# 32 of 512 latent tokens moved from the dense expert products to gathered rows, routing cut into steps, and some VectorE operands read from PSUM

## The reference, cut to what matters

```python
q = (xb @ w_pq).reshape(TOK_BLOCK, 8, 2, 128)
s = einsum('thcd,hcnd->thcn', q, sub_keys)              # 2 x 128 scores for each head
s1, i1 = top_k(s[:, :, 0], 16); s2, i2 = top_k(s[:, :, 1], 16)
top_s, pos = top_k(all 256 sums s1 + s2, 16)            # an expert is i1 * 128 + i2
g = softmax(top_s)
a = gelu(einsum('thk,td->thk', u_exp[eidx], xb))
y = einsum('thk,thkd->td', g * a, v_exp[eidx])
```

## Time and profile before

| what | before |
|---|---|
| median of three runs | 4217.21 us |
| the profiled execution | 4209.3 us |
| its span in the profile | 4207.5 us |
| TensorE busy | 4015.6 us |
| VectorE busy | 2789.8 us |
| GpSimd busy | 2321.4 us |
| ScalarE busy | 1751.2 us |
| moved by DMA | 921.99 MB |

### The profile page before, as it was taken

How to read it: one execution, slowest core, us unless ns; L and a number is a source line. 1 busy time by engine, 2 the same in 40 slices (tenths; PEclk the granted TensorE clock), 3 DMA queues, 4 the chain that set the end, 5 groups by cost and what they waited for, 6 DMA issues and landing times.

```text
span 4207.5 us, 57280 instructions
## 1 busy us (share of the span) xinstructions
PE 4015.6 (95%) x21230; PEld 3364.7 (80%) x21230; DVE 2789.8 (66%) x4311; ACT 1751.2 (42%) x3014; POOL 2321.4 (55%) x1112
## 2 busy tenths in 40 slices
PE   7978999999999899999989999999999989999997
PEld 5757898888888788877769989888888878887875
DVE  3773239889898566566643322989989867676665
ACT  3264324756657322322231132374655732222223
POOL 1101225676767666666643322576676767666664
PEclk9999999999999999999999999999999999999999
DMA  5303235867768988888844312486776898888884
GB/s 207 113 1 126 86 101 165 280 224 244 261 222 284 315 280 288 277 282 286 297 145 180 102 59 88 146 294 216 256 251 226 277 321 275 284 286 276 289 295 157
DMA packets 385364, 921.99 MB, mean 219 GB/s; under 512 B 29296, under 2 KB 161136, under 8 KB 370800
## 3 DMA queue, kind: packets, MB, share of 16 engines
q1 hardware_dynamic: 310432, 647.48, 46.0%
q0 software_dynamic: 73728, 268.47, 18.8%
q10 hardware_dynamic: 976, 3.15, 0.2%
HBM read 776.64 MB, written 142.34 MB: 218 GB/s over the span
## 4 chain that ended last, share of the span: by engine, by line
PE 32%; issue 30%; POOL 29%; DVE 4%; DMA 3%; ACT 1%; DVEq 0%; POOLq 0%; ACTq 0%
PE PS L736 21%; POOL SL L427 17%; POOL ROWS L434 9%; PE PS L544 5%; PE PS L728 4%; POOL SL L418 3%; DMA ROWS<-u_exp,EI 2%; PE PS L748 2%; DMA ROWS<-v_exp,EI 1%; PE PS L695 1%; DVE OH L1196 1%; DVE ROWS L1205 1%; DVE EQ L1177 0%; DVE EQ L1173 0%; ACT SH L963 0%
## 5 line engine op out<-in xcount | busy, mean ns | idle before, releaser
L427 POOL TENSOR_TENSOR SL<-RW,SH 128x1024 fp32r<-128x1024 f32 x512 | 1409.3, 2753 | 922.7 <-ACT SH L963 901.1
L963 ACT CAST SH<-RW 128x1024 fp32r<-128x1024 f32 x512 | 537.4, 1050 | 1063.8 <-PE PS L736 537.7
L736 PE MATMUL PS<-HH,SH 128*128 128x512 f32 x2048 | 815.9, 398 | 28.3 <-POOL SL L427 28.2
L748 PE MATMUL PS<-WH,SH 128*128 128x512 f32 x2048 | 811.2, 396 | 11.0 <-DVE WL L1255 5.6
L748 PE MATMUL PS<-WL,SH 128*128 128x512 f32 x2048 | 809.4, 395 | 0.0
L748 PE MATMUL PS<-WH,SL 128*128 128x512 f32 x2048 | 809.4, 395 | 0.0
L736 PE MATMUL PS<-HL,SH 128*128 128x512 f32 x2048 | 801.5, 391 | 0.0
L736 PE MATMUL PS<-HH,SL 128*128 128x512 f32 x2048 | 801.4, 391 | 0.0
L1211 DVE SCALAR_TENSOR_TENSOR ACC<-ROWS,AA,ACC 128x1024 f32<-128x1024 f32 x256 | 369.7, 1444 | 528.8 <-DMA ROWS<-v_exp,EI 522.3
L418 POOL TENSOR_TENSOR SL<-RW,SH 128x1024 fp32r<-128x1024 f32 x84 | 202.6, 2416 | 816.5 <-ACT SH L788 816.5
L1196 DVE TENSOR_TENSOR OH<-CO,PK 128x1024 f32<-128x1024 f32 x256 | 575.7, 2290 | 96.1 <-PE PS L728 88.0
(11 more groups left out here) (161 smaller groups left out, 5203.4 us busy)
## 6 DMA issues: line engine op xcount, KB each, us to landing
RW<-u_blk SPq DMA_DIRECT2D x256, 512.0 KB
RW<-v_blk SPq DMA_DIRECT2D x256, 512.0 KB
gate_acts<-GE SPq DMA_DIRECT2D x256, 256.0 KB
router_weights<-GT SPq DMA_DIRECT2D x64, 1024.0 KB, 5.2
GB<-router_weights SPq DMA_DIRECT2D x32, 2048.0 KB, 12.3
GL<-gate_acts SPq DMA_DIRECT2D x256, 256.0 KB
RW<-wstream SPq DMA_DIRECT2D x100, 512.0 KB
AW<-wpairs SPq DMA_DIRECT2D x40, 1024.0 KB, 5.1
```

Source lines behind the costliest of these rows:

```text
L427: nc.gpsimd.tensor_tensor(SL[:, r % 2], RW[:, r % RAW], SH[:, r % 2].bitcast(F32), ALU.subtract).then_inc(raw_used, 1)
L736: last = mm(PS[:, n % 2], w[:, n % 2, j], a[:, j, 0:NS], start=(j == 0 and q == 0), stop=(j == DJ - 1 and q == 2))
L748: last = mm(PS[:, dj], w[:, k % 2, dj], a[:, k], start=start, stop=stop)
L963: nc.scalar.copy(SH[:, r % 2], RW[:, r % RAW]).then_inc(hi_done, 1)
```

## The change

- The first 32 latent tokens leave the dense path: `u_product`, `v_products`, gelu, weights and their transfers work on columns 32 to 511, and there are 120 quads instead of 128.
- These tokens are gathered. They are laid out four times over the 128 partitions (32 tokens x 4 groups), so that 32 gathers (`PG`) of 128 rows fetch their 128 picks; a layer now has 160 gathers in each stage (`NPICK`) instead of 128, the new ones first. ScalarE's queue issues eight small DMAs (`few_tokens`) that spread their indices and gates. The v rows add up in `HTOK`; after the last v product TensorE folds the four groups into columns 0 to 31 (`FOLD`), and VectorE waits for that (`folded`).
- Routing becomes a generator of 26 steps that VectorE runs between one-hots and picks, over the blocks of `ROUTE_SPAN`. Quads and gathers are spread evenly (`QUAD_BLOCK`, `PICK_AT`, `VPICK_AT`).
- The numbers 0 to 127 (`IOTA_PS`), the prompt tokens (`HTOK_PS`) and the slot's indices (`IF`) now lie in PSUM, where VectorE reads them. ScalarE's copy of the prompt tokens ahead of the first block goes away; a copy of the 32 tokens comes after `high(0)`.

The core of the diff:

```diff
+NG = 32
+ND = NS - NG
+GQ = P // NG
+PG = PICKS // GQ
+NPICK = PICKS + PG
+NQ = ND // 4
+NTG = ND // TG
...
-OH_BLOCKS = 16
-LEAD, BETWEEN = (20, 20), 12
-SEG = [[LEAD[l] + t * (OH_BLOCKS + BETWEEN) for t in range(TT - 1)] for l in range(DEPTH)]
-OH_AT = [{SEG[l][t] + j: t * OH_BLOCKS + j for t in range(TT - 1) for j in range(OH_BLOCKS)} for l in range(DEPTH)]
-PICKS_AT = [{11: 0, **{SEG[l][t]: t for t in range(1, TT - 1)}} for l in range(DEPTH)]
-EXP_AT = [{9: 0, 19: 1, **{SEG[l][t] - 3: t + 1 for t in range(1, TT - 1)}} for l in range(DEPTH)]
-VPICK_AT = sorted(list(range(2, NB_E)) + [NB_E // 2, NB_E // 2 + NB_E // 4])
-C_MEAN, C_HEAD, C_SWAP, C_ID, C_IOTA, C_SEL, C_COS, C_SIN = 0, 128, 256, 384, 512, 640, 648, 1160
-C_ALL = 1672
+ROUTE_STEPS = 26
+ROUTE_SPAN = ((0, 1), (11, 28), (28, 45), (45, 68), (68, 91))
+EXP_AT = {9: 0, 25: 1, 42: 2, 65: 3, 88: 4}
+PICKS_AT = {12: 0, 46: 1, 69: 2, 92: 3}
+def _spread(a, b, k):
+    return [a + (b - a) * i // k for i in range(k)]
+def tile_of(g):
+    return (NG + 4 * g) // P
+def token_of(g):
+    return (NG + 4 * g) % P
+QUAD_BLOCK = _spread(13, 45, (P - NG) // 4) + _spread(47, 70, 32) + _spread(70, 93, 32) + _spread(93, 119, 32)
+QUADS_AT = [[g for g in range(NQ) if QUAD_BLOCK[g] == n] for n in range(NB_E)]
+PICK_AT = (_spread(20, 28, 9) + _spread(28, 45, 21) + _spread(45, 68, 36) + _spread(68, 91, 36)
+           + _spread(91, 127, NPICK - 102))
+VPICK_AT = _spread(2, NB_E, NPICK)
...
-    J16 = IOTA[:, 0:TOPK]
+    HTOK_PS = PSf[:, 1024:2048]
+    IOTA_PS = PSf[:, 2048:2048 + NKEY]
+    J16 = IOTA_PS[:, 0:TOPK]
+    IF = PSf[:, 2176:2176 + HC * TOPK].rearrange("p (i k) -> p i k", k=TOPK)
     SEL = CO[:, C_SEL:C_SEL + 2]
+    FOLD = CO[:, C_SEL:C_SEL + NG]
...
-            def gather(table, first, p):
-                n = l * 2 * PICKS + first + p
+            def gather(table, first, s):
+                n, c = (l * 2 + first) * NPICK + s, (s + PICKS) % NPICK
                 pool.wait_ge(row_used, n + 1)
                 pool.sem_inc(rows_asked)
                 nc.gpsimd.indirect_dma_start(
                     ROWS[:, n % RING], None, table[l],
-                    bass.IndirectOffsetOnAxis(ap=EI[:, p:p + 1], axis=0)).then_inc(row_in[n % RING], 16)
+                    bass.IndirectOffsetOnAxis(ap=EI[:, c:c + 1], axis=0)).then_inc(row_in[n % RING], 16)
...
+                for s in range(NPICK):
+                    if PICK_AT[s] == n + 1:
+                        if s == 0:
+                            pool.wait_ge(few_in, 16 * 2 * GQ * (l + 1))
+                            pool.wait_ge(rows_free, l + 1)
+                        if s == PG:
+                            pool.wait_ge(ei_done, l + 1)
+                        gather(u_exp, 0, s)
...
+            pe.wait_ge(sc_done, 2 + l * HC + N_PQ - 1)
+            last = mm(IOTA_PS, ID, IOTA, start=True, stop=True)
             last.then_inc(ht_ps, 1)
+            pe.wait_ge(sc_done, 2 + l * HC + N_PQ)
+            pe.wait_ge(few_copied, l + 1)
+            for j in range(DJ):
+                last = mm(PSf[:, 3072 + j * P:3072 + (j + 1) * P], ACC[:, j * P:(j + 1) * P], ID, start=True, stop=True)
+            last.then_inc(few_ps, 1)
...
-                        last = mm(PS[:, n % 2], w[:, n % 2, j], a[:, j, 0:NS],
+                        last = mm(PS[:, n % 2, NG:NS], w[:, n % 2, j], a[:, j, NG:NS],
...
-                            last = mm(PS[:, dj], w[:, k % 2, dj], a[:, k], start=start, stop=stop)
+                            last = mm(PS[:, dj, NG:NS], w[:, k % 2, dj], a[:, k, NG:NS], start=start, stop=stop)
...
+                for g in QUADS_AT[n]:
+                    if g == 0:
+                        pe.wait_ge(few_done, l + 1)
+                    quad(g)
...
+            pe.wait_ge(fold_ready, l + 1)
+            for dj in range(DJ):
+                last = mm(PS[:, dj, 0:NG], HTOK[:, dj * P:(dj + 1) * P], FOLD, start=True, stop=True)
+            last.then_inc(folded, 1)
...
+            nc.scalar.copy(ACC[:].rearrange("p (j g t) -> p j g t", g=GQ, t=NG),
+                           H[:, :, 0:NG].unsqueeze(2).to_broadcast([P, DJ, GQ, NG])).then_inc(few_copied, 1)
...
-            act.wait_ge(ht_ps, l + 1)
-            nc.scalar.copy(HTOK[:], PSf[:, 1024:2048]).then_inc(ht_done, 1)
...
+            def few_tokens():
+                act.wait_ge(pick_ready, l * 4 + 1)
+                g_picks = G[:].rearrange("p h k -> p (h k)")
+                for g in range(GQ):
+                    to, at = slice(g * NG, (g + 1) * NG), slice(g * PG, (g + 1) * PG)
+                    act.dma_start(EI[to, PICKS:NPICK], EI[0:NG, at]).then_inc(few_in, 16)
+                    act.dma_start(WW[to, PICKS:NPICK], g_picks[0:NG, at]).then_inc(few_in, 16)
             high(0)
+            act.wait_ge(few_ps, l + 1)
+            nc.scalar.copy(HTOK[:], PSf[:, 3072:4096]).then_inc(few_done, 1)
...
+            yield from top16(V16, I16, lambda i: SC[:, slot, i], lambda i: SC[:, slot, i], HC, 4)
+            v.tensor_copy(IF, I16[:])
...
+            if n % TT == 1:
+                dve.wait_ge(few_in, 16 * 2 * GQ * (n // TT + 1))
...
-                v.tensor_tensor(OH[:, par], IOTA.unsqueeze(1).unsqueeze(1).to_broadcast(shape),
+                v.tensor_tensor(OH[:, par], IOTA_PS.unsqueeze(1).unsqueeze(1).to_broadcast(shape),
...
+            def u_pick(s):
+                n, c = l * 2 * NPICK + s, (s + PICKS) % NPICK
                 wait_row(n)
-                v.tensor_tensor_reduce(ROWS[:, n % RING], ROWS[:, n % RING], HTOK[:], 1.0, 0.0, ALU.mult, ALU.add,
-                                       AA[:, p:p + 1]).then_inc(row_used, 1)
-            def v_pick(p):
-                n = (l * 2 + 1) * PICKS + p
+                if s == 0:
+                    dve.wait_ge(few_done, l + 1)
+                v.tensor_tensor_reduce(ROWS[:, n % RING], ROWS[:, n % RING], HTOK[:] if s < PG else HTOK_PS,
+                                       1.0, 0.0, ALU.mult, ALU.add, AA[:, c:c + 1]).then_inc(row_used, 1)
...
+                n, c, acc = (l * 2 + 1) * NPICK + s, (s + PICKS) % NPICK, HTOK if s < PG else ACC
                 wait_row(n)
-                v.scalar_tensor_tensor(ACC[:], ROWS[:, n % RING], AA[:, p:p + 1], ACC[:],
+                v.scalar_tensor_tensor(acc[:], ROWS[:, n % RING], AA[:, c:c + 1], acc[:],
...
+                yield from route_halves(l * TT + slot)
+                if slot == 1:
+                    dve.sem_inc(rows_free, 1)
+                yield from route(l * TT + slot, l * 4 + min(slot, max(slot - 1, 1)))
...
-            route_slot(0)
-            route_slot(1)
-            dve.wait_ge(ht_done, l + 1)
-            for t in range(TT - 1):
-                if t > 0:
-                    route_slot(t + 1)
-                    u_picks(range(SEG[l][t] - BETWEEN, SEG[l][t]))
-                dve.wait_ge(pick_done, l * 4 + t + 1)
-                for n in range(SEG[l][t], SEG[l][t] + OH_BLOCKS):
-                    one_hots(2 * OH_AT[l][n])
-                    one_hots(2 * OH_AT[l][n] + 1)
-                    u_picks((n,))
-            u_picks(range(SEG[l][-1] + OH_BLOCKS, NB_E))
+            dve.wait_ge(ht_ps, l + 1)
+            for n in range(NB_E):
+                for slot, (a, b) in enumerate(ROUTE_SPAN):
+                    if n == a:
+                        routing = route_slot(slot)
+                    if a <= n < b:
+                        for step in range(ROUTE_STEPS * (n - a) // (b - a), ROUTE_STEPS * (n - a + 1) // (b - a)):
+                            next(routing, None)
+                for g in QUADS_AT[n]:
+                    if g == 0 or tile_of(g) > tile_of(g - 1):
+                        dve.wait_ge(pick_done, l * 4 + tile_of(g) + 1)
+                    one_hots(g)
+                for s in range(NPICK):
+                    if PICK_AT[s] == n:
+                        u_pick(s)
...
+                        if s == PG - 1:
+                            dve.drain().then_inc(fold_ready, 1)
...
-            dve.wait_ge(v_prod, (l + 1) * NB_E)
+            dve.wait_ge(folded, l + 1)
```

More of the change, by code:

```diff
@@ L355, in experts @@
                     store_gelu(n - 2)
-                if n - 2 in OH_AT[l] and OH_AT[l][n - 2] % 2 == 1:
-                    store_gates(OH_AT[l][n - 2] // 2)
-                if n == last_oh + 3:
+                for tg in range(NTG):
+                    if QUAD_BLOCK[tg * (TG // 4) + TG // 4 - 1] == n - 2:
+                        store_gates(tg)
+                if n == QUAD_BLOCK[-1] + 3:
                     load_gates(0)
@@ L1155, in route_halves @@
             dve.drain()
+            yield
         def route(n, picks_before):
@@ L1178, in route @@
                 dve.drain()
+                yield
                 v.tensor_reduce(I12[:, c], EQ[:], AX_X, ALU.add)
                 dve.drain()
-            if n % TT == 1:
-                v.scalar_tensor_tensor(EI[:], I12[:, 0], float(NKEY), I12[:, 1], ALU.mult, ALU.add).then_inc(ei_done, 1)
+                yield
```

(15 more changed lines are left out.)

140 lines of the change are left out of this document (63 added, 77 removed).

## The result

The changed kernel takes 4146.58 us (median of four runs, 4142.43 to 4156.54) beside 4217.30 us for the one before: a ratio of 0.983, 95% interval 0.982 to 0.985. It is 70.7 us faster; 149 us were forecast. (The kernel before had one more run by then, hence 4217.30 in place of 4217.21 us.) The profiled execution took 4145.56 us, its span is 4143.8 us, 63.7 us under the span of the one before.

The account below looks back on a forecast made before the run. TensorE's matmul starts were taken to pace the kernel. Per layer -56 (u), -19 (v), -1.0 and +1.6 (edges) give -74.4, two layers -149: 4060 us profiled, 4068 us median; 8-in-10 range 4006 to 4150.

Parts of the forecast that it names:

- rival 2: V stage: each two-gather block costs its full 2.2 us, eating the gain; near 4180 us; 4100 to 4200 given 19%.
- Fewer columns: Dense matmuls in u and v: 32 columns fewer save 13.4 ns each, 41 us in each of four stages.
- VectorE in the u stage: PSUM operands bring one-hots to 1.23 us; VectorE barely fits; new u stage 782 us, 56 less.
- rival 3: U stage: PSUM operands relieve nothing, one-hots stay at 2.29 us, u saves nothing or loses 20; 4180 to 4220 us; 4%.
- More gathers: V stage: 32 more gathers are covered on GpSimd, but two-gather blocks lose 22 us; new stage 703 us, 19 less.
- doubles: Blocks with two v gathers: 34 in a stage instead of two, taken at 0.65 us each, at most 2.2.
- its middle case: V stage: two-gather blocks cost 1.2 us each, between the forecast and the full 2.2 us; 4105 us in all.
- rival 4: V stage: DMA load makes gathered rows late in nearly all blocks; 6.25 us a block, about 4260 us, slower; 7%.
- Quads and edges: Eight quads fewer save 7 us a layer; at stage edges the `HTOK` copy saves 1.0 us, the fold adds 1.6.
- the quiet v window: Sign: an undisturbed 40 us window of the v stage should show 183 matmuls.
- `WH` behind `GL`: Sign in the v stage's waits, given as `WH` on `GL`: would name rival 2 and rival 4.
- `OH` late with TensorE waiting: Sign in the u stage: `OH` after `ROWS`, TensorE waiting for scaled one-hots; names rival 3 or VectorE falling behind.

Follow-up runs that it names:

- experiment 9: The changed kernel with one-hots reading their row of indices from SBUF again instead of PSUM; 4183.36 us, ratio 0.993 to the kernel before.
- Experiment 1: The changed kernel with VectorE building each u block's one-hots before its routing steps; 4098.64 us, ratio 0.972 to the kernel before.
- experiment 4: The changed kernel without the 32 added v gathers, with their casts and picks; 4088.17 us, ratio 0.970 to the kernel before.
- experiment 2: The changed kernel with VectorE's `weight` multiplication one block earlier in the v stage; 4129.56 us, ratio 0.979 to the kernel before.
- Experiment 5: The changed kernel with one-hots before routing steps, `weight` a block ahead, and the low weight before the v picks; 4017.28 us, ratio 0.953 to the kernel before.

## Why the prediction was wrong

The median is 79 us above the forecast of 4068, just inside the range (4006 to 4150), in the direction forecast; but the change brought less than half of what I said, and the time lies in the interval that I had given to rival 2 (4100 to 4200). The stages are 84 us above my sum: 44 are stalls in the u stages, 38 stalls in the v stages, and the columns make up the rest. By its steps:

- **Fewer columns**: right in the sum, wrong in each part. I gave a u block 5.14 and a v block 5.28 us; they are 5.23 and 5.20. One slope from 320 to 512 columns misses that the two stages differ at 512 columns: the step to 480 brings 9 ns in u and nearly 17 in v. Over a layer it is +12 us in u and -10 in v, so that the right sum is luck.
- **VectorE in the u stage**: the sizes were right. One-hots have the floor (1.22 against 1.23), GpSimd's u casts 2.45 (under 2.6), VectorE's busy time fell by 120 us. These figures and experiment 9 rule rival 3 out. By the Trainium skill (page "SBUF — State Buffer", section "SBUF: two separate sides") a VectorE operation with two SBUF inputs and a GpSimd operation that reads SBUF exclude each other for a whole instruction, and the traces agree: with one operand in PSUM no one-hot takes over 1.23 us, and with `IOTA` back in SBUF the longest takes 3.43.
- **The failed step** is what I made of it: "VectorE fits, with under 10% to spare, and ScalarE's `gates` sit behind it. So small stalls come where there were none", priced at 2 us in a stage that loses 17.5. Lost are 36 and 43. I compared a block's mean load, 5.9 us, with TensorE's 6.4, and never laid out the order within a block: steps, one-hots, picks. Steps are uneven (26 over 17 or 23 blocks, so two in some), each stands in front of a one-hot, and the picks ahead of them wait for rows. Experiment 1 shows the place of one-hots behind the steps to be the whole difference: with one-hots first 14 and 15 us are lost, which is less than I had.
- **More gathers**: the same failure in the v stage. My 0.65 us for each of 34 doubles, 22 us, is 0.96 us for each of 32 added gathers by experiment 4, 30 us; the stages lose 45 and 47 in all where I had 27. I had followed one chain alone: gather, row, pick, `weight`, `w_high`, cast. It was in part real (8.7 and 10.6 us in experiment 2). But I had read past `weight_low` *behind* the picks in the loop that I quoted, and TensorE waits for it directly. Experiment 5 frees nearly all of it (4 and 3 us are left). Rival 2 named the place and rightly said that doubles cost more: its middle case, 1.2 us each, gives 46 us of loss. But its chain accounts for no more than what experiment 2 gained; rival 4's late rows are real (77 waits of the picks for a row in layer 0's v stage) and harmless once nothing urgent stands behind them.
- **Quads and edges**: as forecast in their sum. It closes: u is 30 and 37 us above my 782, v 7 and 9.5 above 703; together 84 of the 86 us by which the profiled execution, 4145.56 us, is above 4060.
- Of what I said would show it: the one-hots' mean, the casts and the quiet v window (185 touched matmuls where I said 183) did; windows with doubles show 174, 176 and 182, so in the worst of them what I had named for a double's full 2.2 us (175); `WH` behind `GL` and `OH` late with TensorE waiting did too, both named for the rivals.

## What to carry to other kernels

When an engine's program is written out by hand, its share of busy time in a block does not tell whether it delivers in time: write down, for each block, the order of its instructions, which of them can be late (a row from DMA) and who needs what stands behind them. Put what feeds the bound engine first and what only has to be done some time last; here that was worth some 130 us in a kernel with the same work. And test such edits in pairs: moving one instruction up without its input being ready made a new loop that cost 37 us in a stage, and the two together gained 41.
